# Permuting TensorE's stages in the chunk loop of a bidirectional RWKV-7 recurrence

## The chip, the core and the metric

One core of a Trainium2 chip runs the whole encoder layer. The metric is the device time of one execution in microseconds; the median of three runs before is 3397.75 us (3385.12 to 3398.22). The engines run side by side, each through its own instruction list, and meet at semaphores: TensorE (PE in the profile, PEld for its weight loads), VectorE (DVE), ScalarE (ACT), GpSimd (POOL), and SyncE (SP), which here issues the DMAs.

## The reference

A layer of a hybrid encoder on 2048 tokens of 1024 channels: an input projection, in eight heads a recurrence of the RWKV-7 kind in both directions, in eight more banded attention, an output projection, and a gated feed-forward network with a convolution. The change lies in the recurrence alone. For each direction and head it is

```python
def rwkv7_step(S, inp):
    r, w, k, v, a, b = inp
    sa = jnp.einsum('dbhvk,dbhk->dbhv', S, a)
    S = S * w[..., None, :] + sa[..., None] * b[..., None, :] + v[..., :, None] * k[..., None, :]
    y = jnp.einsum('dbhvk,dbhk->dbhv', S, r)
    return S, y
```

with a state S of 64 x 64 per head, carried over all tokens. The outputs y of both directions are added afterwards.

## The kernel before

The kernel runs in phases, one after the other. `recurrence_block` (lines 970 to 1484) works on chunks of L = 64 tokens, NCH = 32 of them in each direction, with four units of two heads (RU = 4). Within a chunk the recurrence is written with products: a triangular system is solved for the chunk, and the state H goes from chunk to chunk. Both directions d = 0 and 1 run through every stage, one behind the other.

All engines run the same loop over slots c. In slot c an engine does stages for the chunk at hand ("now", c), for the next ("ahead", c + 1) and for one eight chunks on ("front", c + LAG). The order inside a slot is a list written out by hand for each engine, and an engine works through its list strictly in that order; a stage starts with its waits (`done`). TensorE's list (lines 1244 to 1248) has eleven stages:

- `x_part(c)` (L1152), products with the state and the values; `u_part(c)` (L1164), the solved system Z times that
- `ak_part(c+1)` (L1190) and `rb_part(c+1)` (L1196), score products of the next chunk
- `h_part(c)` (L1169), the sums for the new state; it waits for `u_copied` and `tok_copied`
- `y_part(c)` (L1178), the outputs, three products per unit, into bank 1; it waits for `rb_masked`, `merged` and `u_copied`
- `tok_part(c+1)` (L1201), the operands b and k turned by products with the identity, into bank 3; `v_part(c+1)` (L1207), the values turned, into bank 3 as well, behind `tok_copied`
- `cross(c+1)` (L1222), products with the solved diagonal blocks, into bank 1; it waits for `spread(c+1)`, `g_copied` and `y_copied` of chunk c, which frees bank 1; `corner(c+1)` (L1232), which waits for ScalarE's copy of `cross`
- `gram(c+8)` (L1212), the matrix whose diagonal blocks will be solved

ScalarE's list (lines 1318 to 1322) is `x_copy(c)`, `u_copy(c)`, `decay`, `tok_copy(c+1)`, `growth`, `spread(c+1)`, `y_copy(c)`, `v_copy(c+1)`, `cross_copy(c+1)`, `gram_copy`. `tok_copy` (L1280) waits for `tok_part`; `spread` (L1286) has three activations per direction and waits for the transposed solutions (`returned`), which VectorE makes once in four chunks (`turn_back`, L1451); `y_copy` (L1298) brings the outputs to `rec_ys`. VectorE scales, masks, sums and decays the state, and merges; GpSimd makes the keys (`keys`, L1334, which waits for the outputs' products of nine chunks earlier) and solves the diagonal blocks. SP issues the loads of the inputs and the stores of `rec_ys`.

In the trace `rec_bank` stands for all the PSUM banks. A stage is recognised by its operands: `rec_akrk,rec_vtok` begins `y_part`, `consts_sb,rec_b` begins `tok_part`, `consts_sb,rec_vin` is `v_part`, `rec_side,rec_g` begins `cross`, `rec_ar,rec_b` is `rb_part` (32 in a row) or begins `gram` (16), `rec_Z,rec_low` begins `corner`, `rec_H,rec_ar` begins `x_part`, `rec_vtok,rec_toks` begins `h_part`. Every product appears as two instructions, so `h_part` has 64 and `y_part` 96.

Of the kernel before, what the change touches and what calls it, by code (L numbers as in the profile page):

```python
# [969 lines left out]
def recurrence_block(nc, K):  # L970
# [15 lines left out]
    LAG = 8  # L986
# [7 lines left out]
    with ExitStack() as ctx:  # L994
# [71 lines left out]
        with nc.Block() as block:  # L1066
# [65 lines left out]
            def _(pe):  # L1132
# [109 lines left out]
                for c in SLOTS:  # L1242
                    now, ahead, front = live(c), live(c + 1), live(c + LAG)
                    for go, stage, n in ((now, x_part, c), (ahead, ak_part, c + 1), (now, u_part, c),
                                         (ahead, rb_part, c + 1), (now and c < NCH - 1, h_part, c),
                                         (ahead, tok_part, c + 1), (now, y_part, c), (ahead, v_part, c + 1),
                                         (ahead, cross, c + 1), (front, gram, c + LAG),
                                         (ahead, corner, c + 1)):
                        if go:
                            for d in DIRS:  # L1250
                                stage(n, d)
# [1038 lines left out]
```

## Time and profile before

| | |
|---|---|
| median of 3 runs | 3397.75 us |
| profiled execution | 3392.86 us |
| its span, first to last instruction | 3391.0 us |
| TensorE / VectorE / ScalarE / GpSimd busy | 90 / 46 / 32 / 24% |
| chunks of the recurrence in the span | 1041 to 1577 us |
| mean granted TensorE clock | 0.958 |

The profile comes from one execution. Times in it are microseconds from the first instruction; a timeline row gives start and duration, engine, line of the kernel, operation, output and inputs, partitions x elements, and how many equal instructions it merges; in brackets is the idle time of the engine before it and what ended it. The granted clock is a share of TensorE's full 2.4 GHz: 1.00 or 0.50. TensorE's matmuls are pipelined, so the starts of the weight loads (PEld) show best when a stage begins.

### The profile page before, as it was taken

To read this page: it belongs to the slowest core of one execution; us is meant where nothing else is said; L and a number is where in the kernel's file an instruction comes from. 1 tells how busy PE (TensorE), PEld (TensorE's weight loads), DVE (VectorE), ACT (ScalarE), POOL (GpSimd) and SP (SyncE) were. 2 spreads that over 40 slices of the span, in tenths; PEclk is the share of its full clock that TensorE was granted. 3 is DMA by queue.
4 is the path that set the end of the run, shared out by engine and by line. 5 is a ranking of instruction groups with operands and counts; after the bars stand their busy time and mean duration, and the time that the engine had idled before them with its cause. 6 is when DMAs were issued, how large, how long until landed. Compare 5 with 4: busy or idle time off the path is not lost. (4 is left out here: it accounts for less than half of the span.)

```text
span 3391.0 us, 64118 instructions
## 1 busy us (share of the span) xinstructions
PE 3053.2 (90%) x26764; PEld 2452.2 (72%) x26764; DVE 1544.3 (46%) x1959; ACT 1070.4 (32%) x2041; POOL 797.0 (24%) x937
## 2 busy tenths in 40 slices
PE   7879989997928899997899599999999999799999
PEld 4554548885527899996566478888888888588887
DVE  4555533333854555542543544444444444333433
ACT  4435541113623444433333321111111111222222
POOL 4434530001656666641222600000000000000000
PEclk9989999998958999998999799999999999899999
DMA  3331122331763333323463411111111111621220
GB/s 112 130 87 36 35 58 58 72 74 39 291 225 108 99 110 106 97 84 101 156 197 119 143 50 49 49 42 39 49 49 49 49 49 37 244 98 50 96 99 35
DMA packets 209174, 311.47 MB, mean 92 GB/s; under 512 B 63193, under 2 KB 134233, under 8 KB 205874
## 3 DMA queue, kind: packets, MB, share of 16 engines
q1 hardware_dynamic: 207506, 307.02, 28.0%
q8 instruction: 171, 2.80, 0.3%
q10 hardware_dynamic: 1440, 1.18, 0.1%
q14 instruction: 57, 0.47, 0.0%
HBM read 208.16 MB, written 99.99 MB: 91 GB/s over the span
## 5 line engine op out<-in xcount | busy, mean ns | idle before, releaser
L91 PE MATMUL up_p<-h_hi,up_w_hi 128*128 128x512 f32 x1408 | 549.0, 390 | 41.8 <-DVE h_lo L1995 38.8
L92 PE MATMUL up_p<-h_lo,up_w_hi 128*128 128x512 f32 x1408 | 548.4, 389 | 0.0
L93 PE MATMUL up_p<-h_hi,up_w_lo 128*128 128x512 f32 x1408 | 548.3, 389 | 0.0
L1947 ACT COPY up_raw<-up_p 128x512 f32<-128x512 f32 x176 | 103.1, 588 | 748.1 <-PE up_p L93 748.1
L91 PEld LDWEIGHTS up_p<-h_hi,up_w_hi 128*128 128x128 f32 x1408 | 264.7, 188 | 99.8 <-issue 44.9
L93 PEld LDWEIGHTS up_p<-h_hi,up_w_lo 128*128 128x128 f32 x1408 | 264.8, 188 | 55.1
L92 PEld LDWEIGHTS up_p<-h_lo,up_w_hi 128*128 128x128 f32 x1408 | 264.8, 188 | 54.6
L91 PE MATMUL down_p<-down_act_hi,down_w_hi 128*128 128x512 f32 x704 | 274.7, 390 | 23.2 <-DVE down_act_lo L2152 23.2
L2005 DVE TENSOR_SCALAR up_con<-up_raw,vecs_sb 128x2048 f32<-128x2048 f32 x44 | 59.3, 1348 | 514.1 <-ACT up_raw L1947 514.1
L92 PE MATMUL down_p<-down_act_lo,down_w_hi 128*128 128x512 f32 x704 | 274.4, 390 | 0.0
L93 PE MATMUL down_p<-down_act_hi,down_w_lo 128*128 128x512 f32 x704 | 274.3, 390 | 0.0
L2149 DVE TENSOR_TENSOR down_w_lo<-down_w,down_w_hi 128x1024 fp32r<-128x1024 f32 x88 | 107.8, 1225 | 309.5 <-ACT down_w_hi L2131 309.5
L2131 ACT CAST down_w_hi<-down_w 128x1024 fp32r<-128x1024 f32 x88 | 92.8, 1055 | 353.5 <-PE down_p L93 334.4
L91 PE MATMUL p_rwkv<-h_hi,rwkv_project_w_hi 128*128 128x512 f32 x448 | 175.4, 392 | 10.3 <-DVE rwkv_project_w_lo L716 10.3
L92 PE MATMUL p_rwkv<-h_lo,rwkv_project_w_hi 128*128 128x512 f32 x448 | 175.2, 391 | 0.0
L93 PE MATMUL p_rwkv<-h_hi,rwkv_project_w_lo 128*128 128x512 f32 x448 | 175.0, 391 | 0.0
L91 PEld LDWEIGHTS down_p<-down_act_hi,down_w_hi 128*128 128x128 f32 x704 | 132.6, 188 | 51.1 <-issue 23.6
L92 PEld LDWEIGHTS down_p<-down_act_lo,down_w_hi 128*128 128x128 f32 x704 | 132.6, 188 | 27.6
L93 PEld LDWEIGHTS down_p<-down_act_hi,down_w_lo 128*128 128x128 f32 x704 | 132.5, 188 | 27.5
L1358 POOL TENSOR_TENSOR rec_part<-rec_W,rec_V 128x31 f32<-128x31 f32 (+15 forms) x248 | 132.0, 532 | 57.6 <-issue 40.3
L529 POOL TENSOR_SCALAR attention_prob<-attention_prob,attention_inv 128x384 f32<-128x384 f32 (+1 forms) x96 | 117.0, 1233 | 121.1 <-DVE attention_inv L595 121.1
L1362 POOL TENSOR_TENSOR rec_V<-rec_V,rec_part 128x31 f32<-128x31 f32 (+15 forms) x248 | 140.2, 565 | 19.4
(232 smaller groups left out, 6292.3 us busy)
## 6 DMA issues: line engine op xcount, KB each, us to landing
rec_inp<-gate_chunks SPq DMA_DIRECT2D x64, 512.0 KB, 3.5
up_w<-in_w_up SPq DMA_DIRECT2D x44, 512.0 KB, 4.0
act_out<-up_con SPq DMA_DIRECT2D x22, 1024.0 KB, 4.3
down_act<-act_out SPq DMA_DIRECT2D x88, 256.0 KB, 2.7
gate_chunks<-gates_out SPq DMA_DIRECT2D x4, 4096.0 KB, 12.1
first_w<-in_w_attn SPq DMA_DIRECT2D x24, 512.0 KB, 3.9
rkv_chunks<-rwkv_project_mix SPq DMA_DIRECT2D x12, 1024.0 KB, 6.4
gate_chunks<-gates_out SPq DMA_DIRECT2D x4, 3072.0 KB, 11.8
```

The lines of the kernel that those rows point to most:

```text
L91: pe.matmul(out, w_hi, x_hi, start=start, stop=False)
L92: pe.matmul(out, w_hi, x_lo, start=False, stop=False)
L93: return pe.matmul(out, w_lo, x_hi, start=False, stop=stop)
L529: ops.tensor_scalar(prob[:, i % PB, lo:hi], prob[:, i % PB, lo:hi], inv[:, b % 2, h:h + 1], None, ALU.mult).then_inc(S[name], 1)
L1358: tt(product, W[:, below, b].unsqueeze(2).to_broadcast([P, n, b + 1]), V[:, b, cols].unsqueeze(1).to_broadcast([P, n, b + 1]), ALU.mult).t ...
L1362: op = tt(V[:, below, cols], V[:, below, cols], product, ALU.add)
L1947: nc.scalar.copy(raw[:, half, 1 + n * NT:1 + (n + 1) * NT], p_u[:, half, n]).then_inc(S["copied_" + c], 1)
L2005: nc.vector.tensor_scalar(con[:, half], raw[:, half, 1:T + 1], cw(1, half, j), cb(half, j), ALU.mult, ALU.add).then_inc(S["c0" + c], 1)
L2131: nc.scalar.copy(w_hi[:, k % 2], w[:, k]).then_inc(S["w_hi"], 1)
L2149: nc.vector.tensor_tensor(w_lo[:, k % 2], w[:, k], w_hi[:, k % 2].bitcast(F32), ALU.subtract).then_inc(S["w_lo"], 1)
```

## The change

In TensorE's list `y_part(c)` moves ahead of `tok_part(c+1)`, directly behind `h_part(c)`. `cross(c+1)` follows `tok_part`, and `v_part(c+1)` comes behind `cross`. The order before is h, tok, y, v, cross, gram, corner; the order after is h, y, tok, cross, v, gram, corner. Both directions of each stage move together. No wait, no product and no list of another engine changes.

```diff
@@ -1243,8 +1243,8 @@
                     now, ahead, front = live(c), live(c + 1), live(c + LAG)
                     for go, stage, n in ((now, x_part, c), (ahead, ak_part, c + 1), (now, u_part, c),
                                          (ahead, rb_part, c + 1), (now and c < NCH - 1, h_part, c),
-                                         (ahead, tok_part, c + 1), (now, y_part, c), (ahead, v_part, c + 1),
-                                         (ahead, cross, c + 1), (front, gram, c + LAG),
+                                         (now, y_part, c), (ahead, tok_part, c + 1), (ahead, cross, c + 1),
+                                         (ahead, v_part, c + 1), (front, gram, c + LAG),
                                          (ahead, corner, c + 1)):
                         if go:
                             for d in DIRS:
```

## Rows read from the trace of the kernel before

**Rows 1.** The page: busy time of each engine, and the queue that brings instructions.

```profile
PE 3053.2 (90%) x26764; PEld 2452.2 (72%) x26764; DVE 1544.3 (46%) x1959; ACT 1070.4 (32%) x2041; POOL 797.0 (24%) x937
...
q8 instruction: 171, 2.80, 0.3%
```

**Rows 2.** Stretch: length, busy (count) PE, PEld, DVE, ACT, POOL; clock, DMA share, GB/s.

```profile
1041.22:1577.16 535.94, 502.08 (x15590) 495.10 (x15589) 260.91 (x570) 232.01 (x698) 308.41 (x538) 0.98 0.30 95
```

**Rows 3.** Waits from 1040 to 1540: waiter and releaser, total us, times, longest.

```profile
POOL rec_b L1337 <- PE rec_bank L1138: 74.4, 14, 10.6
...
PE rec_bank L1138 <- issue: 18.6, 25, 2.9
...
PE rec_bank L1138 <- ACT rec_ys L1301: 10.5, 8, 1.9
...
PE rec_bank L1149 <- issue: 4.4, 9, 1.2
```

**Rows 4.** Timeline of TensorE's weight loads, one slot: start us, duration, stage.

```profile
1259.92 0.20 PEld L1138 LDWEIGHTS rec_bank<-rec_vtok,rec_toks 64*64 64x64 f32 x4
...
1261.78 0.55 PEld L1149 LDWEIGHTS rec_bank<-consts_sb,rec_b 64*64 64x64 f32 x16
...
1263.65 0.20 PEld L1138 LDWEIGHTS rec_bank<-rec_akrk,rec_vtok 64*64 64x64 f32 x4
...
1266.45 1.02 PEld L1149 LDWEIGHTS rec_bank<-consts_sb,rec_vin 64*64 64x64 f32 x32
1267.38 0.55 PEld L1138 LDWEIGHTS rec_bank<-rec_side,rec_g 64*64 64x64 f32 x16
...
1268.32 0.55 PEld L1138 LDWEIGHTS rec_bank<-rec_ar,rec_b 64*64 64x64 f32 x16
...
1269.25 0.55 PEld L1138 LDWEIGHTS rec_bank<-rec_Z,rec_low 64*64 64x64 f32 x16
...
1270.18 0.20 PEld L1138 LDWEIGHTS rec_bank<-rec_H,rec_ar 64*64 64x64 f32 x4
```

**Rows 5.** Timeline of ScalarE in the same slot.

```profile
1263.92 0.58 ACT L1283 COPY rec_toks<-rec_bank 128x512 f32<-128x512 f32 x1 [0.35 <-PE rec_bank L1149]
1264.40 0.72 ACT L1277 ACTIVATE rec_grow<-rec_inp 128x256 f32<-128x256 f32 x2
1265.03 0.68 ACT L1293 ACTIVATE rec_Z<-rec_upper,rec_masks 128x128 f32<-128x128 f32 x2
...
1266.78 0.62 ACT L1301 COPY rec_ys<-rec_bank 128x256 f32<-128x256 f32 x2
1267.29 0.73 ACT L1306 COPY rec_vtok<-rec_bank 128x256 f32<-128x256 f32 x2
...
1268.56 0.27 ACT L1311 COPY rec_low<-rec_bank 128x128 f32<-128x128 f32 x1 [0.20 <-PE rec_bank L1138]
```

**Rows 6.** Groups by line from 1040 to 1540: busy us, mean ns of one.

```profile
L1301 ACT COPY rec_ys<-rec_bank 128x256 f32<-128x256 f32 x56 | 17.8, 359 | 2.6 <-PE rec_bank L1138 2.6
```

**Rows 7.** Timelines of a slot with turned solutions: VectorE, ScalarE, TensorE.

```profile
1242.64 0.42 DVE L1422 TENSOR_TENSOR rec_H<-rec_bank,rec_H 128x256 f32<-128x256 f32 x1 [1.92 <-PE rec_bank L1138]
...
1245.48 2.03 DVE L1456 STREAM_TRANSPOSE rec_lower<-rec_V 128x1024 f32<-128x1024 f32 x1
...
1249.32 0.62 ACT L1301 COPY rec_ys<-rec_bank 128x256 f32<-128x256 f32 x2
...
1249.92 0.66 PE L1138 MATMUL rec_bank<-rec_side,rec_g 64*64 64x32 f32 x16 [1.72 <-ACT rec_ys L1301]
...
1254.23 0.23 PEld L1138 LDWEIGHTS rec_bank<-rec_H,rec_ar 64*64 64x64 f32 x4
```

**Rows 8.** Stretches, columns as in rows 2: behind two gaps before `cross`.

```profile
1250.60:1254.00 3.40, 3.40 (x71) 3.40 (x68) 1.20 (x4) 0.74 (x3) 0.00 (x0) 0.50 0.48 152
...
1457.80:1459.90 2.10, 0.47 (x16) 0.34 (x10) 0.00 (x0) 2.10 (x9) 0.94 (x2) 1.00 0.00 0
```

**Rows 9.** Timeline of TensorE's weight loads: an idle time inside `h_part`.

```profile
1489.91 0.18 PEld L1138 LDWEIGHTS rec_bank<-rec_us,rec_toks 64*64 64x64 f32 x2 [3.08 <-issue]
```

## The prediction

> **What bounds the kernel now.** I read the page first: TensorE is busy 90% of the span, the other engines at most 46% [rows 1]. Next come the stretches, because a mean over phases says nothing of one phase. The products of the recurrence fill 535.94 us, from 1041.22 to 1577.16, and there TensorE is busy 502.08 us, VectorE 260.91, ScalarE 232.01 and GpSimd 308.41 [rows 2]. So the chunks are bound by TensorE's own issue order, and an edit of that order can gain at most the idle 34 us and lose whatever it uncovers. The waits of this phase say what the idle time is: 10.5 us in 8 places until ScalarE's copy of the outputs (`rec_ys`), and 18.6 + 4.4 us on issue, which no semaphore explains [rows 3].
>
> Then one chunk in order of time. The slot from 1254.23 to 1270.18 takes 15.95 us and has no dependency wait on TensorE. The stages follow each other: `h_part` at 1259.92, `tok_part` 1261.78 to 1263.65, `y_part` to 1266.45, `v_part` to 1267.38, `cross` to 1268.32, `gram` to 1269.25, `corner` to 1270.18 [rows 4]. ScalarE in the same time runs one unbroken chain: the two `tok_copy` (1263.92 the second), `growth`, the six activations of `spread`, the two `y_copy`, the two `v_copy`, `cross_copy` [rows 5]. The reader should see that `cross` starts at 1267.38, just after the first `y_copy` has ended: 1266.78 + 0.36, the mean of one such copy [rows 6], is 1267.14. `cross` waits for that copy, because it writes the same bank as `y_part`. ScalarE issues the copy behind `tok_copy`, `growth` and `spread`, so it comes late whenever `y_part` itself ended.
>
> **The change part by part.** Nothing is removed or added: all products, copies and semaphores stay, and only TensorE's list is permuted; the lists of ScalarE, VectorE, GpSimd and SP are untouched. No DMA moves on its queue.
>
> 1. `y_part` ahead of `tok_part`. It needs `rb_masked`, `merged` and `u_copied`. `h_part` has just waited for the last, `u_part` for `merged`, and the mask of `rb` follows within a microsecond of `rb_part`, while `h_part` takes 1.86 us (1259.92 to 1261.78) [rows 4]. So it starts without a wait: cost 0. If the mask were late, the price would be its own copy, some 0.4 us. What is gained is nothing directly: the reader of the outputs is ScalarE, whose copy stays where it stood in its queue.
>
> 2. `tok_part` 2.80 us later (the length of `y_part`, 1263.65 to 1266.45 [rows 4]). This is the edit that costs. Its products release `tok_copy`, and behind that wait ScalarE has queued `growth`, `spread`, `y_copy`, `v_copy` and `cross_copy`: the whole chain of [rows 5] moves later by 2.80 us against the slot's start.
>
> 3. `cross` directly behind `tok_part`, so `y_part` and `v_part` no longer lie between them. Before, these two gave TensorE 1267.38 - 1263.65 = 3.73 us of work while ScalarE went from the second `tok_copy` to the first `y_copy`. That chain takes the same time: from the end of `tok_part`'s issue, 1263.65, to 1267.14, plus the way of a semaphore. That way I take from another slot: there `y_copy` began at 1249.32 and would end its first copy at 1249.68, and `cross` started at 1249.92 [rows 7], so 0.2 us. 1267.14 + 0.21 - 1263.65 = **3.7 us of idle TensorE in each slot**. The second direction's copy is 0.26 us later and lies under the first direction's 0.47 us of cross products: 0. `v_part`, `gram` and `corner` are queued behind the waiting `cross`, on the same engine, and can't fill the gap. The bounds: 3.5 (no semaphore latency) and 3.9.
> There are 31 such slots (chunks 0 to 30). In seven of them `spread` waits for VectorE's transposes of the solved blocks before it starts, which is what most of the 8 waits of 10.5 us are [rows 3, 7]. After the change this wait is absorbed: the transposes begin after the state's sums, whose place in the slot is unchanged, and end some 5 us after `h_part`: in the slot of [rows 7] the last sum starts at 1242.64, 0.3 us behind `h_part`, and the second transpose ends at 1247.51; `tok_part` alone now ends 2.80 + 1.87 = 4.7 us after it, and two copies and `growth` follow. So the sum is 31 x 3.7 = 114.7, less 10.5 = **104.2 us**; with 3.5 and 3.9 it is 98 to 110.
>
> 4. `v_part` behind `cross`. Its copy now stands late: `v_copy` precedes `cross_copy` on ScalarE, and `corner` waits for the latter. With X the start of `cross`: `v_part` ends at X + 1.87, its last copy at about X + 2.1 + 0.4, the two `cross_copy` (0.27 each) at X + 2.75 and X + 3.0, while `gram` ends at X + 2.8. So `corner` waits 0.1 to 0.3 us, before it waited 0 (1269.25 follows `gram` directly [rows 4], the second copy of `cross` ended at 1268.83 [rows 5]). I take 0.1 x 31 = **3 us**, between 0 and 9. The next `x_part` needs `v_copied` about X + 2.5 and starts at X + 3.8: hidden. The very first chunk waits for its values' copy, about **1 us** once.
>
> 5. TensorE's clock. After the gap of 1.72 us that `cross` shows in the slot of [rows 7], the granted clock is 0.50 (the 1.2 GHz level) from 1250.60 to 1254.00 [rows 8], and the work from `cross` to the end of `corner` takes 1254.23 - 1249.92 = 4.31 us where at 2.4 GHz it takes 1270.18 - 1267.38 = 2.80 [rows 4, 7]: 1.5 us lost. Such a stretch follows four of the gaps before `cross` (at 1250.6, 1322.3, 1393.9 and 1530.5); the one at 1457.80 has no such fall, clock 1.00 [rows 8]. A gap of 3.7 us is twice as long as any of these, so I take one fall for each slot: (31 - 4) x 1.5 = **40.5 us**. Bounds: 0, if none were added, and twice 1.5 for each slot, 93, if two stretches followed.
> The Trainium skill, in TensorE: Matmul & The Clock Gate (Part 1), says that the half clock is the resting state, that an idle engine returns to it and sustained work lifts it again; the trace has both levels as said, and by that rule every slot pays.
>
> 6. The idle time on issue, 23.0 us here [rows 3]. The clearest case is at 1489.91: 3.08 us idle in the middle of one stage, where no wait stands [rows 9]; the page shows instructions arriving by a DMA queue of their own [rows 1]. While TensorE is held 3.7 us, some of these arrivals are covered. Between 0 and 23 us come back; I take a quarter, **-6**, since the stall is at one place of the slot and such gaps are at several.
>
> Sum: 104 + 3 + 1 + 40.5 - 6 = 143 us. The profiled execution was 3392.86 us (span 3391.0), so it would become 3536. The median of the runs is 5 us above it, 3397.75, and their spread is 13 us; I put the forecast at 3538. About 0.5% (17 us) is what a measurement of this kernel can tell from no change.
>
> **The rivals.**
> A. As summed: 3538 us. For it speaks the unbroken ScalarE chain [rows 5].
> B. The same stall, but the clock falls no oftener than now: 104 + 4 - 6 = 102, so 3500 us. For it: half of the gaps before `cross` had no fall behind them. Against it: the new ones are twice as long.
> C. Each gap brings the half clock twice, before its end and after it: 31 x 1.5 = 46 more, 3584 us. For it only the length of the gap.
> D. TensorE runs `v_part` and `gram` past the waiting `cross`. These are 1.87 us (0.93 each [rows 4]), so the stall would be 1.8: 31 x 1.8 - 10.5 = 46, so 3444 us. Against it: in [rows 7] the products of `gram`, whose operands were long there, didn't start in the gap. The Trainium skill (TensorE: Matmul & The Clock Gate, Part 3, The mechanism) says that weight loads may be pulled ahead while matmuls keep strict order; the gap agrees.
> E. No difference, 3398 us: the copies of the outputs leave ScalarE's queue early, so that nothing is uncovered. That the change doesn't do what it says would end here. Against it: that queue's order is fixed, and the copy stands behind `tok_copy`.
> F. **Faster.** `y_part` ends 1.9 us sooner after `h_part`, and GpSimd stood 74.4 us before `keys` until the outputs' products [rows 3]. If the keys and with them the loads came sooner, off the instruction fetches, the 23.0 us on issue and the 10.5 us before `cross` could go: 3398 - 33 = 3365 us. It decides only if the new stall stays under 33 / 31 = 1.1 us in a slot; the chain above makes it 3.7. Against it as well: GpSimd is busy 308 of 536 us and TensorE never waits for it in steady slots.
>
> **How the numbers follow.** A 0.62, B 0.17, C 0.09, D 0.05, E 0.03, F 0.03, with 0.01 for something else that is slower. The predicted time is A's. The range runs from a little under B (less all of the issue time back: 3490) to between A and C, 3575; D, E, F and C's upper part lie outside, 0.2 together. A's terms alone give 3515 to 3560. Faster 0.03 (F), same 0.03 (E), slower 0.94.
>
> **What would show it.** In the profile after: TensorE's wait for `rec_ys` grows from 10.5 to about 115 us in 31 places near 3.7 us; slots of some 21 us instead of 15.95 to 17.3; `y_part` starts directly behind `h_part`; the granted clock of the recurrence falls from 0.98 to about 0.9, with a half-clock stretch for each slot; ScalarE's wait before `rec_toks` grows while its chain from there to `rec_ys` keeps 3.2 us; no longer stages anywhere else. What would make it wrong: a gap clearly under 3 us (another engine gave cover), or the clock staying at 1.00.

## The result and the profile after

The changed kernel takes 3543.28 us (3540.91 to 3549.69, four runs) against 3397.98 us before: ratio 1.0443, interval 1.0425 to 1.0461. It is 145 us slower, and the forecast was 3538. The profiled span is 3539.0 us instead of 3391.0.

Stretch of the chunks in the changed kernel, to be laid beside [rows 2] (length, then busy time and count of PE, PEld, DVE, ACT and POOL, granted clock, DMA share, GB/s):

```profile
1041.07:1724.28 683.21, 564.92 (x15592) 557.98 (x15589) 252.84 (x571) 227.97 (x700) 303.37 (x538) 0.87 0.24 75
```

The chunks take 683.21 us instead of 535.94, 147.3 more: the whole loss lies here. The same number of products keeps TensorE busy 62.8 us longer (564.92 against 502.08), which is the clock, and its idle time grows from 33.9 to 118.3 us, which is waiting. The other engines have as much work as before.

What TensorE waited for in that stretch (total us, times, longest), after:

```profile
PE rec_bank L1138 <- ACT rec_ys L1301: 103.8, 31, 3.6
PE rec_bank L1138 <- issue: 7.5, 13, 1.1
PE rec_bank L1138 <- ACT rec_low L1311: 4.4, 7, 0.6
PE rec_bank L1138 <- DVE rec_akrk L1402: 1.4, 2, 1.2
PE rec_bank L1149 <- issue: 1.2, 1, 1.2
```

The wait for the copy of the outputs went from 10.5 us in 8 places to 103.8 us in 31, one per slot. The idle time on issue fell from 23.0 to 8.7 us. `corner` now waits for the copy of `cross` (`rec_low`), 4.4 us in all.

One slot (1085.41 to 1106.42), first TensorE's weight loads, then ScalarE, answering to [rows 4] and [rows 5]:

```profile
1092.76 0.23 PEld L1138 LDWEIGHTS rec_bank<-rec_akrk,rec_vtok 64*64 64x64 f32 x4
...
1095.56 0.58 PEld L1149 LDWEIGHTS rec_bank<-consts_sb,rec_b 64*64 64x64 f32 x16
...
1101.14 0.57 PEld L1138 LDWEIGHTS rec_bank<-rec_side,rec_g 64*64 64x64 f32 x16 [3.61 <-issue]
...
1102.36 1.88 PEld L1149 LDWEIGHTS rec_bank<-consts_sb,rec_vin 64*64 64x64 f32 x32
1104.06 1.03 PEld L1138 LDWEIGHTS rec_bank<-rec_ar,rec_b 64*64 64x64 f32 x16
...
1106.42 0.23 PEld L1138 LDWEIGHTS rec_bank<-rec_H,rec_ar 64*64 64x64 f32 x4
```

```profile
1096.78 0.58 ACT L1283 COPY rec_toks<-rec_bank 128x512 f32<-128x512 f32 x1 [5.54 <-PE rec_bank L1149]
1097.71 0.58 ACT L1283 COPY rec_toks<-rec_bank 128x512 f32<-128x512 f32 x1 [0.35 <-PE rec_bank L1149]
1098.19 0.72 ACT L1277 ACTIVATE rec_grow<-rec_inp 128x256 f32<-128x256 f32 x2
1098.82 0.68 ACT L1293 ACTIVATE rec_Z<-rec_upper,rec_masks 128x128 f32<-128x128 f32 x2
...
1100.57 0.61 ACT L1301 COPY rec_ys<-rec_bank 128x256 f32<-128x256 f32 x2
1103.61 0.37 ACT L1306 COPY rec_vtok<-rec_bank 128x256 f32<-128x256 f32 x1 [2.43 <-PE rec_bank L1149]
```

The outputs' products (`rec_akrk,rec_vtok`) were all issued at 1095.56, but their copy starts at 1100.57, because ScalarE stood 5.54 us at `tok_copy` and then had to do `growth` and `spread`. From the second `tok_copy` to the start of `rec_ys` are 1100.57 - 1097.71 = 2.86 us, exactly as in [rows 5] (1266.78 - 1263.92). Only the work of TensorE that lay beside this chain has gone. The first row of TensorE after the gap is a weight load and says "issue"; the matmul behind it names the releaser:

```profile
1101.18 0.66 PE L1138 MATMUL rec_bank<-rec_side,rec_g 64*64 64x32 f32 x16 [3.50 <-ACT rec_ys L1301]
```

And the clock behind such gaps (columns as above), where before only four of the gaps had a fall behind them [rows 8]:

```profile
1101.70:1105.10 3.40, 3.40 (x71) 3.40 (x69) 0.00 (x0) 1.00 (x4) 2.77 (x9) 0.50 0.36 114
1122.20:1129.00 6.80, 6.80 (x129) 6.80 (x130) 1.65 (x5) 1.60 (x6) 1.31 (x3) 0.50 0.24 80
1651.30:1661.50 10.20, 9.48 (x166) 9.32 (x168) 0.58 (x2) 1.92 (x7) 0.00 (x0) 0.50 0.17 55
```

After the gap of this slot 3.4 us run at 0.50, the 1.2 GHz level, and behind the next slot's gap 6.8 us do. The clock falls in each of the 31 slots: 13 stretches at 0.50 last 3.4 us, 16 last 6.8 us, and two near the end last 10.2 us, 172 us of half clock in all. In the kernel before, the chunks have 18 us of it.

### The profile page after: what moved, and what is told of

It reads as the page before. It is cut to its first block and busy times, and to the rows that moved or that the text cites. A ratio compares the mean times of both kernels' runs of the same rounds, so it can differ in the third digit from the quotient of the medians.

```text
span 3539.0 us, 64118 instructions
## 1 busy us (share of the span) xinstructions
PE 3115.0 (88%) x26764; PEld 2516.1 (71%) x26764; DVE 1535.7 (43%) x1959; ACT 1065.3 (30%) x2041; POOL 792.5 (22%) x937
## 5 line engine op out<-in xcount | busy, mean ns | idle before, releaser
L91 PE MATMUL p_rwkv<-h_hi,rwkv_project_w_hi 128*128 128x512 f32 x448 | 175.3, 391 | 10.2 <-DVE rwkv_project_w_lo L716 10.2
L1435 DVE TENSOR_SCALAR rec_E<-rec_bank,rec_masks 128x128 f32<-128x128 f32 x64 | 22.5, 351 | 299.2 <-PE rec_bank L1138 298.2
```

Of the source, the lines that this page charges most:

```text
L91: pe.matmul(out, w_hi, x_hi, start=start, stop=False)
L1435: nc.vector.tensor_scalar(E[:, problems(f, d)], bank[d][2][:, :, 0:BL], half(0), None, ALU.mult).then_inc(S["diag_a"][d], 1)
```

## The experiments

The kernel before was run again beside each of them: 3394.93 us beside the first four, 3396.16 us beside the last three. The ratios are to these.

**ScalarE's copy first.** The changed kernel with `y_copy` ahead of `tok_copy` in ScalarE's list.

```diff
-                                         (ahead, tok_copy, c + 1), (after, growth, c + LAG + 1),
-                                         (ahead, spread, c + 1), (now, y_copy, c), (ahead, v_copy, c + 1),
+                                         (now, y_copy, c), (ahead, tok_copy, c + 1), (after, growth, c + LAG + 1),
+                                         (ahead, spread, c + 1), (ahead, v_copy, c + 1),
```

> The changed kernel with one edit in ScalarE's list: `y_copy` stands ahead of `tok_copy`. Theory (the cost is ScalarE's chain from `tok_copy` to the copy that frees bank 1): `cross` now waits for the first direction's `spread` instead, which in the kernel before ended at 1265.61 + 0.39 = 1266.00, so the gap is 1266.00 + 0.21 - 1263.65 = 2.55 us instead of 3.71; 31 x 1.15 = 36 us less, and some half-clock time less: 3490 to 3508 us. Rival (the new order of the products costs by itself, whatever ScalarE does): gap 3.7, 3543 us. Rival (only the outputs' copy matters): gap 0, about 3400 us.

Measured: 3486.88 us, ratio 1.0273 (1.0255 to 1.0290). `cross` now waits for `spread`:

```profile
1099.09 0.65 PE L1138 MATMUL rec_bank<-rec_side,rec_g 64*64 64x32 f32 x16 [2.18 <-ACT rec_side L1295]
1099.97 0.66 PE L1138 MATMUL rec_bank<-rec_Z,rec_g 64*64 64x32 f32 x16 [0.22 <-ACT rec_side L1295]
```

The gap changes its releaser and shrinks to 2.18 us, with 0.22 more for the second direction, which the expectation had overlooked. TensorE's waits before `cross` fell from 103.8 to 68.9 us, as expected, and its busy time in the chunks from 564.92 to 543.64 us, with 20 falls of the clock instead of 31. The total is 3 us better than the theory's range. The cost is what stands in ScalarE's list ahead of the copy, and the outputs' copy alone is not all of it.

**The spread and the outputs' copy first.** The changed kernel, with everything that `cross` needs from ScalarE's list ahead of `tok_copy`.

```diff
-                                         (ahead, tok_copy, c + 1), (after, growth, c + LAG + 1),
-                                         (ahead, spread, c + 1), (now, y_copy, c), (ahead, v_copy, c + 1),
+                                         (ahead, spread, c + 1), (now, y_copy, c), (ahead, tok_copy, c + 1),
+                                         (after, growth, c + LAG + 1), (ahead, v_copy, c + 1),
```

> The changed kernel, ScalarE's list as decay, `spread`, `y_copy`, `tok_copy`, growth, `v_copy`. Theory: in three slots of four nothing that `cross` waits for stands behind `tok_copy`, so the gap is 0 there and the slot returns to some 16 to 17 us. In the seven slots in which the solutions are turned, `spread` can begin only 5.2 us after `h_part`, takes 2.1 us and the first `y_copy` 0.36: the gap is 7.9 - 4.7 = 3.2 us there, with a half-clock stretch. Against the kernel before 7 x (3.2 - 1.7) + 3 x 1.5 = 15 us more, less what the issue time gives: 3400 to 3420 us. Rival (the order of the products costs by itself): over 3500 us.

Measured: 3406.61 us, ratio 1.0037 (1.0024 to 1.0050), with TensorE's list exactly that of the changed kernel. In a slot without turned solutions there is no gap left, and `cross` follows `tok_part` 0.47 us behind its last group of loads:

```profile
1232.42 0.58 PEld L1149 LDWEIGHTS rec_bank<-consts_sb,rec_k 64*64 64x64 f32 x16
1232.89 0.58 PEld L1138 LDWEIGHTS rec_bank<-rec_side,rec_g 64*64 64x64 f32 x16
```

TensorE's waits over the chunks are

```profile
PE rec_bank L1138 <- issue: 18.3, 30, 2.9
PE rec_bank L1138 <- ACT rec_ys L1301: 16.2, 7, 2.6
```

so the wait for the outputs' copy is left in the seven slots with turned solutions, 2.3 us each where 3.2 were expected. This refutes that the new order of the products costs much by itself: 137 of the 145 us go with a permutation of ScalarE's list. The 12 us that remain over the kernel before are clear of the noise. The waits for `rec_ys` are 6 us longer than there, `corner` waits 4.5 us, and TensorE is busy 10 us longer in the chunks, with some 35 us at the half clock instead of 18.

**One stage of cover given back.** The changed kernel with `v_part` ahead of `cross` again.

```diff
-                                         (now, y_part, c), (ahead, tok_part, c + 1), (ahead, cross, c + 1),
-                                         (ahead, v_part, c + 1), (front, gram, c + LAG),
+                                         (now, y_part, c), (ahead, tok_part, c + 1), (ahead, v_part, c + 1),
+                                         (ahead, cross, c + 1), (front, gram, c + LAG),
```

> The changed kernel with `v_part` back ahead of `cross` (order h, y, tok, v, cross, gram, corner). Theory (these stages are cover and nothing else): the gap shrinks by `v_part`'s length, 3.71 - 0.93 = 2.78 us, and `corner` waits nowhere: 31 x 0.93 + 6 = 35 us less, 3508 us; with fewer half-clock stretches down to 3490. Rival (the whole loss is the clock that falls once in each slot): 3543 less little, since the fall stays.

Measured: 3475.97 us, ratio 1.0237 (1.0217 to 1.0257), lower than expected.

```profile
PE rec_bank L1138 <- ACT rec_ys L1301: 61.9, 31, 2.3
...
PE rec_bank L1149 <- ACT rec_toks L1283: 6.3, 30, 0.2
```

```profile
1055.56 0.66 PE L1138 MATMUL rec_bank<-rec_side,rec_g 64*64 64x32 f32 x16 [2.15 <-ACT rec_ys L1301]
...
1075.45 1.06 PE L1138 MATMUL rec_bank<-rec_side,rec_g 64*64 64x32 f32 x16 [2.15 <-ACT rec_ys L1301]
```

```profile
1055.56:1059.00 3.44, 3.44 (x118) 3.44 (x119) 1.67 (x7) 1.60 (x7) 3.28 (x6) 1.00 0.52 155
1075.40:1081.80 6.40, 6.34 (x119) 6.38 (x121) 2.42 (x8) 1.66 (x7) 5.77 (x10) 0.50 0.29 86
...
1041.00:1658.00 617.00, 535.73 (x15576) 524.93 (x15574) 255.31 (x570) 227.29 (x698) 304.82 (x538) 0.93 0.26 83
```

The waits fell by 103.8 - 61.9 - 6.3 = 36 us and by 4 for `corner`, as expected. The rest is the clock: TensorE is busy 535.73 us, so the half clock costs 34 us over the kernel before instead of 63. The gaps are 2.15 us in the slots with `growth` and 1.53 in the last eight, with 0.2 us more in front of `v_part`. The clock falls in 18 slots of 31, where it fell in all 31 with gaps of 2.9 to 3.5 us; the rows show two gaps of 2.15 us, one without a fall and one with it. What decides between them is not shown. The expectation held this at 0 to 18 us, and it was 29. The rival, that the clock falls in each slot all the same, is out.

**The gap filled.** The changed kernel with products of constants in the gap (`FILL` is 4), so that TensorE waits no longer but works for nothing.

```diff
+                def fill(c, d):
+                    done(pe, "rb_masked", d, c + 2)
+                    wide = K.consts[:, 0:RU * L].rearrange("p (u t) -> p u t", u=RU)
+                    for _ in range(FILL):
+                        for rows in HALVES:
+                            pe.matmul(bank[d][2][rows, :, L:], ident[rows, rows], wide[rows], start=True, stop=True)
...
-                                         (now, y_part, c), (ahead, tok_part, c + 1), (ahead, cross, c + 1),
+                                         (now, y_part, c), (ahead, tok_part, c + 1), (now and ahead, fill, c), (ahead, cross, c + 1),
```

> The changed kernel with 16 products of 64 x 64 by 256 columns between `tok_part` and `cross` (constants by constants, into bank 2, overwritten by `gram`); they belong to no part of the computation. At 2.4 GHz they take some 3.4 us, the length of the gap. Theory (61 of the 145 us are the clock, paid because TensorE is idle): the gap before `cross` shrinks to 0.3 us at an unchanged start of `cross`, the granted clock of the recurrence returns to 0.97 or more, and the time falls by 45 to 60 us to 3483 to 3498. Rival (the half clock does not depend on the gap, or costs nothing as the slot waits for ScalarE anyway): 3543 us or more.

Measured: 3490.83 us, ratio 1.0278 (1.0261 to 1.0296).

```profile
1098.16 3.22 PEld L1247 LDWEIGHTS rec_bank<-consts_sb 64*64 64x64 f32 x32
1101.87 0.57 PEld L1139 LDWEIGHTS rec_bank<-rec_side,rec_g 64*64 64x64 f32 x16 [0.48 <-issue]
...
1117.94 3.62 PE L1247 MATMUL rec_bank<-consts_sb 64*64 64x256 f32 x31
1121.60 0.66 PE L1139 MATMUL rec_bank<-rec_side,rec_g 64*64 64x32 f32 x16
```

```profile
1041.00:1676.00 635.00, 609.74 (x16676) 576.48 (x16676) 254.23 (x575) 229.37 (x704) 304.18 (x538) 0.99 0.26 81
```

`cross` starts as late as in the changed kernel, 1101.87 - 1098.16 = 3.7 us behind `tok_part`, and still the time is 52 us lower, since the clock is 0.99 instead of 0.87: it falls once in these slots and not 31 times. Useless work makes the kernel faster than idling: this is the price of the clock, measured with the chain untouched. It is a lower bound, for the idle time on issue rose again to 16.4 + 0.9 us in this kernel, 8.6 more than in the changed one.

**The smaller swap on the kernel before.**

```diff
-                                         (ahead, tok_part, c + 1), (now, y_part, c), (ahead, v_part, c + 1),
-                                         (ahead, cross, c + 1), (front, gram, c + LAG),
+                                         (ahead, tok_part, c + 1), (now, y_part, c), (ahead, cross, c + 1),
+                                         (ahead, v_part, c + 1), (front, gram, c + LAG),
```

> The kernel before with one swap: `cross` ahead of `v_part` (order h, tok, y, cross, v, gram, corner), so that only `y_part`'s 2.80 us lie between `tok_part` and `cross`. Theory: the 0.93 us of `v_part` were cover in full, since in the kernel before `cross` started just as its copy was there: 31 x 0.9 = 28 us, 6 us of `corner` waiting in the last slots, which have no `gram`, and 3 to 10 us of half clock: 3430 to 3445 us. Rival (a gap under 1 us is absorbed by the idle time on issue): 3400 us.

Measured: 3424.46 us, ratio 1.0084 (1.0066 to 1.0102), a little under the theory's range.

```profile
PE rec_bank L1138 <- ACT rec_ys L1301: 29.5, 26, 2.6
PE rec_bank L1138 <- issue: 12.2, 18, 1.8
PE rec_bank L1149 <- issue: 6.6, 9, 1.8
PE rec_bank L1138 <- ACT rec_low L1311: 4.4, 7, 0.6
```

The wait for the copy grew by 19 us where 28 were expected. In the slots with `growth` the matmul's row shows a new wait of 0.70 us, 0.2 less than the gap as in the changed kernel, so the 0.9 us of `v_part` came there; in the last ones without it at most 0.23 us did:

```profile
1146.78 0.66 PE L1138 MATMUL rec_bank<-rec_side,rec_g 64*64 64x32 f32 x16 [0.70 <-ACT rec_ys L1301]
...
1519.30 0.66 PE L1138 MATMUL rec_bank<-rec_Z,rec_g 64*64 64x32 f32 x16 [0.23 <-ACT rec_ys L1301]
```

So the cover was exhausted as read, in most slots: there is no slack between `cross` and the copy that the smaller edit could use.

**More cover where the kernel before still waits.** Only in slots with turned solutions, `gram` goes ahead of `cross` on TensorE, and ScalarE takes `y_copy`, `spread`, `cross_copy`, `v_copy` in this order.

```diff
+                    solved = [(ahead, cross, c + 1), (front, gram, c + LAG)]
+                    if (c + 1) % GROUP == 0:
+                        solved.reverse()
...
+                    own = [(ahead, spread, c + 1), (now, y_copy, c), (ahead, v_copy, c + 1), (ahead, cross_copy, c + 1)]
+                    if (c + 1) % GROUP == 0:
+                        own = [own[1], own[0], own[3], own[2]]
```

> The kernel before with another order in the one slot of four that turns the solutions: TensorE does `gram` ahead of `cross`, ScalarE `y_copy` ahead of `spread` and `cross_copy` ahead of `v_copy`. Theory (the gap of 1.7 us there is lack of cover): cover grows by 0.93 us and the chain shrinks by 0.4 to 0.7, the gap splits into waits of 0.1 to 0.6 us, and the four half-clock stretches go: 7 x 0.5 + 4 x 1.5 = 9 us less than before, about 3387 us, ratio 0.997. Rival (a later `cross` delays `corner` and the merge as much): no difference.

Measured: 3381.39 us, ratio 0.9953 (0.9939 to 0.9966): faster than both kernels, 15 us under the kernel before.

```profile
PE rec_bank L1138 <- issue: 18.9, 26, 2.7
PE rec_bank L1149 <- issue: 4.5, 8, 1.0
PE rec_bank L1138 <- ACT rec_ys L1303: 0.7, 1, 0.7
PE rec_bank L1138 <- ACT rec_side L1297: 0.6, 2, 0.4
```

```profile
1041.00:1562.00 521.00, 495.59 (x15542) 489.21 (x15538) 258.53 (x565) 231.64 (x697) 306.41 (x532) 0.99 0.31 98
```

The 10.5 us of waits became 1.3, and TensorE is busy 6.5 us less, with two stretches at the half clock instead of five. Together this is more than the 9 us that were expected. The same reading that priced the loss gives a gain. The run has the edits of both lists at once, so it does not tell what each is worth.

**The loads made small.** The kernel before, with most of each load of the recurrence's inputs left out from the third chunk on, so that its outputs are not the layer's.

```diff
+                        n = RU if f < 2 else 1
-                        sp.dma_start(inp[d][:, f % 2, 0:4 * RU].rearrange("p m t -> p (m t)"),
-                                     gat_dram[:, at, FIRST[d] * RU * L:(FIRST[d] + 4) * RU * L]).then_inc(
+                        sp.dma_start(inp[d][:, f % 2, 0:4 * n].rearrange("p m t -> p (m t)"),
+                                     gat_dram[:, at, FIRST[d] * RU * L:FIRST[d] * RU * L + 4 * n * L]).then_inc(
...
-                                     rkv_dram[:, at, 0:RU * L]).then_inc(S[parity("in", f)][d], 16)
+                                     rkv_dram[:, at, 0:n * L]).then_inc(S[parity("in", f)][d], 16)
```

> The kernel before, in which from the third chunk on each load of the recurrence's inputs brings only a sixteenth or a quarter of its rows (4 of 16 and 1 of 4), so the chunks compute with stale inputs. Theory (TensorE's idle time on issue is its instructions arriving late beside these loads): the 23 us on issue fall under 8, and the time by 15 to 25 us: 3373 to 3383. Rival (it is a price of the instruction stream itself): 23 us stay, 3398 us.

Measured: 3374.25 us, ratio 0.9930 (0.9914 to 0.9946), 22 us less.

```profile
PE rec_bank L1139 <- ACT rec_ys L1302: 12.8, 8, 1.8
PE rec_bank L1139 <- issue: 11.5, 12, 2.9
```

The idle time on issue halved, 23.0 to 11.5 us, but did not fall under 8; the loads of the values and the first quarter's, which remained, may hold the rest. That the loads cause half of it is shown. By which way they delay TensorE, the arrival of instructions above all, is argued from the separate queue in [rows 1] and not shown. The 22 us are more than the 11.5; TensorE is also busy 493.1 us in the chunks instead of 502.1. Less half clock is only a part of that: three stretches of 3.4 us instead of five, some 3.5 us. The rest is open.

## Why the prediction was right

- **Step 1, `y_part` ahead, cost 0.** Right: there is no wait for the mask or the merge before it in the waits above.
- **Steps 2 and 3, the stall.** Right in mechanism, place and size: 3.50 us by the matmul's row (3.61 by the weight load's) where 3.7 stood, in 23 of the 31 places. Less what was there, it is 103.8 - 10.5 = 93 us against the 104 of the sum. The 11 us have two causes. The waits of the rows begin at the modelled end of the matmuls, 0.2 us late. And the last eight slots have no `growth`, because its chunk would lie beyond the last, so ScalarE's chain is shorter there and the rows show 2.9 us instead of 3.5. The list of slots should have been read to its end.
- **The absorbed wait for the transposes [rows 7].** Right: in the slot from 1283.44, one with turned solutions, the weight load of `cross` shows the same idle time as elsewhere:

```profile
1299.17 0.58 PEld L1138 LDWEIGHTS rec_bank<-rec_side,rec_g 64*64 64x64 f32 x16 [3.61 <-issue]
```

- **Step 4, `corner`.** 4.4 us against 3 forecast, but elsewhere than I put it. It is 0.6 us in each of seven of the last slots, which have no `gram` between `v_part` and `corner`, and next to nothing in the others.
- **Step 5, the clock.** The direction was right, and the size too small: 62.8 us more busy time against 40.5, because of the 31 stretches at 0.50 sixteen lasted 6.8 us and two 10.2, where the sum had 3.4 for each. This is the term that was mis-sized most. Rival C was thus true in part, rival B (no more falls than before) is out, and the granted clock fell to 0.87 instead of 0.9. The filled gap gives 52 us for the same thing, 61 with the idle time that came back there.
- **Step 6, the idle time on issue.** -14.3 us against -6: more of it than a quarter was covered while TensorE was held. With the gap filled, 8.6 us of it came back.
- **Rival D** (work running past the waiting `cross`) is refuted by the 31 full gaps. **Rival F** was wrong in its premise too: GpSimd's keys now wait for `growth` on ScalarE, which is as late as `tok_copy`, so earlier outputs free nothing:

```profile
POOL rec_b L1337 <- ACT rec_grow L1277: 173.5, 18, 16.1
```

The terms measured are 93.3 + 4.4 + 1.4 + 62.8 - 14.3 = 147.6 us (1.4 are two waits for the masked scores `rec_akrk`, 1.15 of it in the first slot; the wait for the first values, put at 1 us, is not among the rows), and the stretch is 147.3 us longer. So the total was right to 5 us partly because errors cancelled: the stall was 11 us too high and the issue time gave back 8 us more than forecast, and the clock was 22 too low. That is luck in the size, not in the mechanism. Two figures of the prediction don't follow from its own terms: 143 us on 3397.75 is 3541 and not 3538, and B less all of the issue time is 3398 + 104 + 4 - 23 = 3483 and not 3490. Neither decides anything here.

The Trainium skill's rule of the idle engine that returns to the half clock (TensorE: Matmul & The Clock Gate, Part 1) holds here: the granted clock fell to 0.50 in or right behind each of the 31 gaps of 2.9 to 3.5 us, and the runs give its price.

## What to carry to other kernels

A stage of the bound engine that stands between a producer and its consumer's return is cover, whatever it computes: before moving it, follow the other engine's list from the wait that the moved stage releases to the copy that the next stage needs, and lay its length beside the work that remains between. An engine's in-order list couples things that have nothing to do with each other, so read both lists before permuting one. Price an idle gap of TensorE at more than its length: here each of 3.5 us cost two more at the half clock.

## What the runs showed that was not expected

Filling an idle gap with 3.6 us of useless products made the kernel 52 us faster, at one and the same start of the next useful product. And the clock does not fall with every gap: with gaps of 2.9 to 3.5 us it fell in each slot and cost 63 us of busy time over the chunks, with 1.5 to 2.15 us in 18 slots of 31 and cost 34. Set against the waits that were added, 93 us and 58, that is 0.7 us for each of them in the first kernel and 0.6 in the second.
